# Streaming-encoder trunk on one core: row sums ahead of splits at the mixer's end, GpSimd's third weight combination ahead of a normalisation factor, and one matrix for the meta tokens

## What is computed

```python
h = jnp.concatenate([meta, x], axis=1)                    # 16 + 2048 rows of 1024
u = (h @ w_in).reshape(b, t, 4, 256)                      # pooling windows 2, 4, 8, 16
pooled = trailing mean of u over the group's window
y = jnp.einsum('btgc,gce->btge', pooled - u, w_group).reshape(b, t, 1024)
m = (y * scale) @ w_out
h = layer_norm(ALPHA * h + m, ln_mix_g, ln_mix_b)         # ALPHA = 2 ** 0.25
gate, up = jnp.split(h @ w_gu, 2, axis=-1)                # 2 x 2816 columns
f = (jax.nn.silu(gate) * up) @ w_down
h = layer_norm(ALPHA * h + f, ln_ffn_g, ln_ffn_b)
return h[:, 16:]
```

## Time and profile before

| | us |
|---|---|
| median of 3 runs (1656.8 to 1665.4) | 1661.54 |
| profiled execution | 1657.87 |
| its span, first to last instruction | 1656.1 |
| TensorE (PE) busy | 1639.9 (99%) |
| VectorE (DVE) busy | 1050.9 (63%) |
| GpSimd (POOL) busy | 649.1 (39%) |
| ScalarE (ACT) busy | 616.5 (37%) |
| waits of PE for other engines, all six of the list together | 8.7 |

### The profile page before, as it was taken

One profiled execution on the slowest core, in us unless ns is written; L12 is line 12 of the kernel. 1 busy time (PEld: TensorE's weight loads), 2 busy tenths in 40 slices (PEclk: granted clock), 3 DMA queues, 4 the chain that ended last, 5 costly groups with the idle time before them and its releaser, 6 DMA issues.

```text
span 1656.1 us, 19058 instructions
## 1 busy us (share of the span) xinstructions
PE 1639.9 (99%) x7318; PEld 1355.9 (82%) x7318; DVE 1050.9 (63%) x1085; ACT 616.5 (37%) x836; POOL 649.1 (39%) x439
## 2 busy tenths in 40 slices
PE   8999999999999999999999999999999999999998
PEld 7888888877888888888888888888888888888886
DVE  6779876987444444445756676776644434467866
ACT  5334465446333333333533333333333332322220
POOL 0440025015347666654456566666631000341002
PEclk9999999999999999999999999999999999999999
DMA  9674378444357566565656666666668543564542
GB/s 342 245 289 167 130 260 299 175 147 183 115 165 235 190 204 226 181 223 190 228 176 205 220 217 212 191 205 197 193 205 289 176 156 128 196 223 172 201 141 94
DMA packets 190954, 330.84 MB, mean 200 GB/s; under 512 B 8464, under 2 KB 132496, under 8 KB 181136
## 3 DMA queue, kind: packets, MB, share of 16 engines
q1 hardware_dynamic: 151168, 297.64, 52.4%
q10 hardware_dynamic: 37520, 23.60, 4.7%
q0 software_dynamic: 2176, 8.39, 1.3%
HBM read 227.36 MB, written 102.24 MB: 199 GB/s over the span
## 4 chain that ended last, share of the span: by engine, by line
PE 94%; DVE 2%; POOL 1%; DMA 1%; issue 1%; ACT 1%; SPq 0%; POOLq 0%; DVEq 0%; ACTq 0%
PE acc L1227 42%; PE acc L1256 19%; PE acc L1060 11%; PE turn L1227 7%; PE turn L1256 6%; PE acc L1094 5%; PE turn L1094 3%; DMA raw<-w_out 1%; PE turn L1048 1%; PE acc L1137 1%; DVE stats L1753 0%; DVE wf L1823 0%; DVE split L1777 0%; POOL rstd L889 0%; POOL wr L883 0%
## 5 line engine op out<-in xcount | busy, mean ns | idle before, releaser
L1227 PE MATMUL acc<-fa,wf 128*128 128x512 f32 x1584 | 366.6, 390 | 2.3 <-DVE acc L1942 1.7
L1227 PE MATMUL acc<-fb,wf 128*128 128x512 f32 x1584 | 363.4, 389 | 0.4 <-DVE acc L1942 0.4
L1227 PEld LDWEIGHTS acc<-fb,wf 128*128 128x128 f32 x1584 | 297.1, 188 | 63.0 <-issue 1.4
L1227 PEld LDWEIGHTS acc<-fa,wf 128*128 128x128 f32 x1584 | 295.8, 188 | 64.3 <-DVE wf L1823 3.0
L1256 PE MATMUL acc<-dw,da 128*128 128x512 f32 x1386 | 315.3, 389 | 0.0
L1256 PEld LDWEIGHTS acc<-dw,da 128*128 128x128 f32 x1386 | 260.1, 188 | 54.0
L1823 DVE TENSOR_TENSOR wf<-wt,wf 128x512 fp32r<-128x512 f32 x132 | 139.9, 1061 | 157.0 <-ACT wf L1428 156.6
L1823 DVE TENSOR_TENSOR wf<-wr,wf 128x512 fp32r<-128x512 f32 x176 | 177.7, 1014 | 51.4 <-ACT wf L1428 51.0
L883 POOL TENSOR_TENSOR wt<-wr,wt 128x512 f32<-128x512 f32 x88 | 136.1, 1546 | 169.4 <-DVE wf L1823 169.2
L1428 ACT CAST wf<-wr 128x512 fp32r<-128x512 f32 x176 | 108.6, 618 | 210.4 <-PE acc L1227 204.9
L1060 PE MATMUL acc<-mov,split 128*128 128x512 f32 x768 | 177.5, 391 | 0.0
(11 more groups left out here) (138 smaller groups left out, 1807.6 us busy)
## 6 DMA issues: line engine op xcount, KB each, us to landing
wr<-w_gu SPq DMA_DIRECT2D x44, 1024.0 KB, 5.2
dar<-af_dram SPq DMA_DIRECT2D x56, 704.0 KB, 4.4
af_dram<-g ACTq DMA_DIRECT2D x32, 512.0 KB, 5.8
raw<-w_in SPq DMA_DIRECT2D x15, 1024.0 KB, 7.6
fs<-hf_dram SPq DMA_DIRECT2D x14, 1024.0 KB, 5.6
dt_raw<-w_down SPq DMA_DIRECT2D x22, 512.0 KB, 6.0
wt_dram<-dt_t SPq DMA_DIRECT2D x22, 512.0 KB, 4.2
sa<-af_dram SPq DMA_DIRECT2D x22, 512.0 KB, 8.3
```

What stands on the lines that cost most here:

```text
L1227: mm = nc.tensor.matmul(dst, wf[:, slot, a, k, :], fa[half][i][:, v, :, k, :], start=i < 2 and k == 0 and n3 == 0, stop=k == KC - 1 and n3 ...
```

## The change

1. `meta_features`: a new constant `parts` (48 rows and more by 16; GpSimd adds two slices of `ident` at the start) has a one at column j in row j and in row 32 + j. One matmul for each column tile against `parts` takes the place of two against `ident`.
2. VectorE, end of the second half's mixer: the low part of form 3 goes behind the row sums of t = 5. The row sum of t = 6, m = 0, goes between low parts 1 and 2 of unit 0; the other three stay behind low part 3.
3. GpSimd: `rstd_of(3)` goes behind all four T forms of unit 2.

```diff
+        parts = sb("parts", [2 * LO_AT, N_META])
...
+            pool.wait_ge(ident_ready, 1)
+            nc.gpsimd.tensor_tensor(parts[:], ident[0:2 * LO_AT, 0:N_META], ident[0:2 * LO_AT, LO_AT:LO_AT + N_META],
+                                    ALU.add).then_inc(ident_ready, 1)
...
             unit_t4(1)
-            rstd_of(3)
             for n in range(UNITS):
...
                 if n + 2 < UNITS:
                     unit_t4(n + 2)
+                if n == 0:
+                    rstd_of(3)
...
                 if i == 0:
-                    pe.wait_ge(ident_ready, 1)
+                    pe.wait_ge(ident_ready, 2)
...
                 for m in range(2):
-                    for v in range(2):
-                        mm = nc.tensor.matmul(acc[:, 5, m * H:(m + 1) * H], meta_rows[:, m * P:(m + 1) * P],
-                                              ident[0:2 * LO_AT, v * LO_AT:v * LO_AT + N_META],
-                                              start=v == 0, stop=v == 1)
+                    mm = nc.tensor.matmul(acc[:, 5, m * H:(m + 1) * H], meta_rows[:, m * P:(m + 1) * P], parts[:],
+                                          start=True, stop=True)
...
                     if h and t == NP - 1:
                         form_lo(4)
-                        for q in range(4):
-                            unit_lo(0, q)
+                        unit_lo(0, 0)
+                        unit_lo(0, 1)
+                        add_rows(h, t, (0,))
+                        unit_lo(0, 2)
+                        unit_lo(0, 3)
+                        add_rows(h, t, range(1, TT))
+                        form_lo(5)
...
                     if h:
-                        for q in ((), (0,), (1,), (2,), (), (3,), ())[t]:
+                        for q in ((), (0,), (1,), (2,), (), (), ())[t]:
                             form_lo(q)
-                    if t in (1, 3, 4, 5, 6):
+                    if t in (1, 3, 4, 5) or h == 0 and t == 6:
                         add_rows(h, t)
-                    if h and t == NP - 1:
-                        form_lo(5)
+                    if h and t == 5:
+                        form_lo(3)
```

More of the change, by code:

```diff
@@ L1730, in row_half, with add_rows @@
                 return zm[e][:, m, cols * TOK:(cols + 1) * TOK]
-            def add_rows(h, t):
-                for m in range(TT):
+            def add_rows(h, t, tiles=range(TT)):
+                for m in tiles:
                     rows_ = row_half(h, t, m)
```

## The result

| | before | with the change |
|---|---|---|
| median of 18 runs each | 1657.57 us | 1663.98 us |
| lowest and highest | 1655.81, 1665.40 | 1660.38, 1665.38 |
| profiled execution | 1657.87 | 1664.46 |
| its span | 1656.1 | 1662.6 |

The ratio is 1.0028 with a 95% interval of 1.0018 to 1.0037: the changed kernel is 0.28% slower, 4.6 us (the medians alone are 6.4 apart; the ratio's bounds are 3.0 and 6.1 us). The forecast said 0.3 us faster. It is within the 0.5% that the prediction called the same, but the sign is wrong, and the interval excludes no change. Two runs further down, one of g1 (2368.54) and one of before beside the h runs (1915.69), were slowed by hundreds of us, and the ratios leave them out.

What follows compares the result with a forecast made beforehand. PE, busy 99% of the span, was taken to bound the kernel. The terms -1.98 and +1.7 (holding the mixer's 0.5) gave -0.3, so 1661.2 us from a median of 1661.54; range 1655.0 to 1666.0.

Steps and rivals of the forecast that it cites:

- Meta stages: Four early stages lose half of their 8 PE instructions each: -1.98 us, bounds 1.5 to 2.0.
- PE's early work is a chain of its own products there, so the gain moves everything behind it: Behind the meta stages: their gain of 1.98 us was taken to carry through to all later work.
- Mixer's end: From product 6 to unit 0's product 2: product 0 starts 1.6 earlier, 0.5 us is left; bounds 0 and 2.57.
- first-sight gain of 2.57: Mixer's end: 1.79 before product 6 plus 0.78 before unit 0, a sum that the prediction didn't take.
- Unit 1: PE's wait for `c_seeded`: a later factor moves PE's restart to 414.5 from 412.82, +1.7 us; bounds +0.2 and +4.2.
- The sum: Whole kernel: -1.98 for the meta stages and +1.7 for unit 1 give -0.3 us.
- all cases lie between -6.4 and +4.2: Whole kernel: claimed limits in us of the change's effect over the forecast and its rivals.
- T forms block the statistics: Unit 1: GpSimd's T forms also hold up VectorE's statistics; +2.2 us in all, 1663.7 us; chance 0.18.
- all three waits go: Mixer's end and unit 1: PE's three targeted waits vanish; -6.4 us, 1655.1 us; chance 0.12.
- a late load: Unit 1: unit 2's load lands after low part 3, so nothing collides; -1.6 in all, 1659.9 us; chance 0.2.
- The change doesn't do what it says: Meta stages keep their 0.99 us each, as a fixed time; +1.7, 1663.2 us; chance 0.04.
- 0.96 on the same: Whole kernel: chance 0.96 that the time stays within about 0.5%, 8.3 us, of no change.

Runs made afterwards that it cites:

- g1: Kernel before with VectorE's new order at the mixer's end and `rstd_of(3)` between the third and fourth T forms of unit 2; 1655.06 us, ratio 0.9980.
- h runs: Four kernels that issue the `ss_mix` stores from ScalarE's queue or hold PE back with the meta change; medians 1656.32 to 1661.89 us, before 1660.88.
- i2: Kernel before with a second place for the `ss_mix` sums and the meta-stage change; 1655.50 us, ratio 0.9987.
- i1: Kernel before with a second place for the `ss_mix` sums of steps 1 and 3; 1657.01 us, ratio 0.9989.
- h1: Kernel before with the meta-stage change, and nine idle matmuls at the start of block 1 giving the two microseconds back; 1661.89 us, ratio 1.0011.
- j2: Changed kernel with six of SP's row loads, four of them moved, behind the load issued at 270.6 us; 1657.78 us, ratio 1.0003.
- i4: Changed kernel with a second place for the `ss_mix` sums; 1658.69 us, ratio 1.0002.
- e3: Kernel before with only GpSimd's part, `rstd_of(3)` behind all four T forms of unit 2; 1661.63 us, ratio 1.0024.
- j3: j2 with `rstd_of(3)` between the third and fourth T forms of unit 2, one buffer; 1652.40 us, ratio 0.9973.
- f2: Kernel before with the meta-stage change and eight small matmuls put back at the start; 1659.78 us, ratio 1.0003.
- j1: Changed kernel with SP's pair of row loads put behind the next load of `w_in`; 1661.37 us, ratio 1.0021.
- i3: i1 with the meta-stage change, VectorE's mixer-end order and `rstd_of(3)` between the third and fourth T forms of unit 2; 1653.05 us, ratio 0.9969.
- e2: Kernel before with only VectorE's new order at the mixer's end; 1656.34 us, ratio 0.9990.
- h2: Kernel before with the `ss_mix` stores issued from ScalarE's queue and the meta-stage change; 1658.47 us, ratio 0.9994.
- h0: Kernel before with the four `ss_mix` stores issued from ScalarE's queue instead of GpSimd's; 1660.72 us, ratio 1.0009.
- e4: Changed kernel without the meta-stage change, so VectorE's and GpSimd's parts together; 1661.61 us, ratio 1.0021.
- f1: Kernel before with `parts` and GpSimd's addition made, but the two old matmuls still used; 1658.07 us, ratio 1.0003.

## Why the prediction was wrong

- **Meta stages: right, a little high.** 0.54 for each stage (44.37 to 44.91) where half of 0.99 was forecast, so 1.8 and not 1.98. It came through to the end only where the stores were not in the way: 1.5 in i2 against i1, by the medians.
- **"PE's early work is a chain of its own products there, so the gain moves everything behind it": wrong.** This is the step that failed. It was read from the first 60 us and carried over 240 us in which PE waits for nothing, but in which GpSimd waits 7.93 for a DMA, with 2.1 us left between the last split and PE. The stretch cost 5.0 (2.46 ahead to 2.57 behind). The list of waits could not show it, since PE's idle time there was zero. GpSimd's timeline could: waits of 7.93, 4.58 and 4.33 for a store of its own, with ScalarE and VectorE behind it. Nor was the 2.5 us that the changed kernel stood ahead the trigger (h1); the row loads 0.3 us ahead of the store were (j2). Without this loss the change stands at 1.0002 of before (i4) or 1.0003 (j2), and neither interval excludes the forecast's 0.9998.
- **Mixer's end: right to 0.5 us.** Product 0 of unit 0 was forecast 1.6 earlier than before, in before's own time at 379.3; with the 2.57 taken off it came at 378.82. Product 2 was forecast at 385.9 with a new wait of 1.2 for ScalarE, and came at 385.57 with 1.05. The first-sight gain of 2.57 was rightly refused.
- **Unit 1: right in the replay, wrong in the price.** PE went on at 414.30 in before's time, where 414.5 stood. The term ended at that start. Behind it 48 matmuls took 14.05, 13.43 in i4 and 12.77 in j2 in place of 11.16: 1.6 to 2.9 us that the sum did not have. By medians part 3 alone cost 3.4 (e3), and with the second buffer, where the stretch costs nothing, the change is still 1.7 slower than i1 (i4) where the sum had 0.3 faster.
- **The sum.** -1.98 came as -1.8 (the other 0.7 of the 2.46 is the earlier start) and +1.7 as +1.5 up to PE's start in unit 1; +5.0 (the stretch to 303 us, 1.7 of it the clock) and +2.9 (the clock in unit 1) were missing. The sentence that all cases lie between -6.4 and +4.2 took unit 1's bound for a total; the highest total among the rivals is +2.2.
- **The rival that T forms block the statistics** is refuted: eight statistics took 4.83 with two T forms beside them. That its 1663.7 lies next to the measured 1663.98 is luck. By the rule of the Trainium skill named in the prediction (SBUF — State Buffer, "Who interferes with whom") a VectorE instruction with one SBUF input, outside its two-port modes, doesn't contend with GpSimd, and the trace agrees at 0.60 each. **That all three waits go** is refuted, and so is **a late load**: the first T form did meet low part 3. **The change doesn't do what it says** is refuted by the 0.54. j3 comes near to the first of these, with 0.3, 1.0 and 0.2 left at the places of the three waits, but by a place of the factor that the change does not have.
- **The range.** 0.96 on the same is where the ratio lies, and 1663.98 is inside 1655.0 to 1666.0. But the 1661.2 in the middle stood on a median of three runs of before, 1661.54, and 18 runs gave 1657.57; that the range holds the result is luck in part. The spread of those three runs was taken as one of measurement. At least a part of it is a race between transfers in the kernel: of i1's 12 runs, with the second buffer, two lie above 1660 where 10 of before's 35 do, and of j2's ten none above 1659 where 4 of before's 21 do.

**Open:** why the second row load is held up, and why fewer PE instructions end that. f2's profile speaks for their number; nothing shows the path from there to SP's issue. Open too are the wait for `mov` at 88 us (j1, i2, i3) and what releases `g` late at 595 us in some executions (i1, g1, e2).

## What to carry to other kernels

A stretch in which the bounding engine never waits is not a stretch with slack: look in it for the engine that waits for its own store to a single buffer, and ask how late that store may come. Where one kernel's runs lie several microseconds apart, look for a race inside the kernel before a change of 2 us is judged; here, four loads that nobody needed early were moved, and the ten runs lay within 1.7 us. And cost a wait of PE by the time at which the matmuls behind it are done, not by when the first one starts.

## What the runs showed of the hardware

- **The clock behind a wait.** After PE waits of 3.1 to 4.1 us the 24 or 48 matmuls behind them took 1.4 to 2.9 longer in every profile (7.09 to 8.53 for 24, 12.51 to 14.05 for 48), with a granted clock of 0.50 in the first 3.2 us behind the changed kernel's 3.97. After waits of 1.6 to 2.3 some took their usual time (5.73 in g1 behind 2.00, 5.74 in h2 behind 1.76) and some did not: 7.30 in i1 behind 1.98, 7.35 in h0 behind 1.77, 45.40 in place of 43.82 for 192 in j1 behind 2.30.
- **One transfer, three durations.** The same 1 MB store from the same place was waited for 12.66, 7.93 and 5.59 us, the last with the 1 MB of loads 0.3 us ahead of it gone, the first two with those loads issued in 0.80 and in 1.77 us.
- **Order of issue.** The second store, of the same size, was waited for 4.24 to 4.58 us where it was issued 1.8 us ahead of a 1 MB load on SP's queue (before, e2, e3, e4, g1), and 9.88 and 10.48 where it came 1.5 behind it (f1, f2).
- **Shared access to SBUF.** A VectorE subtraction with two SBUF inputs took 1.79 beside GpSimd and 0.68 alone; GpSimd's took 3.22 and 1.3. Statistics took 0.60 in either case.
